# A two-layer diffusion trunk on one core: first-layer scale columns as full-width matmuls, the shift in halves, the last output tile in token halves

## The reference, cut to what matters

```python
for i in range(2):
    sh, sc, gt = split((silu(cond) @ ada_w[i] + ada_b[i]), 3)   # once for the 512 latent, once for the 256 context tokens
    h = rmsnorm(x, norm_g[i]) * (1 + sc) + sh
    # layer 0: fourier mixer, layer 1: retention mixer (both with a SiLU gate and an output projection)
    o = fourier_mixer(h, w_in, w_out)  if i == 0 else  retention_mixer(...)
    x = x + gt * o
return rmsnorm(x, final_g)              # (1, 512, 1024)
```

## Time and profile before

| | us |
|---|---|
| median of 3 runs | 1000.4 (1000.3, 1000.4, 2994.8) |
| the profiled execution | 998.61 |
| its span on the core | 996.8 |
| PE busy | 941.6 |
| DVE / ACT / POOL busy | 562.2 / 343.6 / 248.3 |

### The profile page before, as it was taken

How to read it: one execution, slowest core, us unless ns; L and a number is a source line. 1 busy time by engine, 2 the same in 40 slices (tenths; PEclk the granted TensorE clock), 3 DMA queues, 4 the chain that set the end, 5 groups by cost and what they waited for, 6 DMA issues and landing times.

```text
span 996.8 us, 12904 instructions
## 1 busy us (share of the span) xinstructions
PE 941.6 (94%) x4748; PEld 810.4 (81%) x4748; DVE 562.2 (56%) x804; ACT 343.6 (34%) x577; POOL 248.3 (25%) x244
## 2 busy tenths in 40 slices
PE   6969998999999999959999999999999999998993
PEld 6968998888888888847888888887888788877882
DVE  6485877899995332358334445426434544565344
ACT  7233334232314332334333334323333323452230
POOL 3337970475574000024100131013100410020001
PEclk9989999999999999989999999999999999998997
DMA  8473332555555211211221122202121121102212
GB/s 307 140 233 152 121 101 90 190 191 173 186 188 206 92 64 64 84 42 56 72 76 52 35 72 69 68 13 84 63 65 40 42 84 42 63 1 89 101 63 84
DMA packets 27864, 98.67 MB, mean 99 GB/s; under 512 B 3848, under 2 KB 4008, under 8 KB 27568
## 3 DMA queue, kind: packets, MB, share of 16 engines
q1 hardware_dynamic: 25792, 90.25, 27.1%
q0 software_dynamic: 2032, 7.89, 2.1%
HBM read 96.01 MB, written 2.10 MB: 98 GB/s over the span
## 4 chain that ended last, share of the span: by engine, by line
PE 87%; DVE 7%; DMA 2%; POOL 2%; ACT 1%; issue 1%; DVEq 0%; SPq 0%; POOLq 0%
PE banks L1541 28%; PE banks L1542 28%; PE banks L1543 27%; DMA raw<-stream 2%; PE banks L1594 2%; DVE hreg L1334 1%; POOL gate L625 1%; DVE xreg L1393 1%; DVE gate L1328 1%; DVE ring L1003 1%; DVE xreg L1533 0%; DVE gate L1358 0%; POOL gate L618 0%; POOL xreg L635 0%; PE banks L1783 0%
## 5 line engine op out<-in xcount | busy, mean ns | idle before, releaser
L1541 PE MATMUL banks<-hreg,ring 128*128 128x512 f32 (+2 forms) x928 | 334.1, 360 | 26.9 <-DVE hreg L1334 9.1
L1542 PE MATMUL banks<-hreg,ring 128*128 128x512 f32 (+2 forms) x928 | 331.8, 358 | 0.0
L1543 PE MATMUL banks<-hreg,ring 128*128 128x512 f32 (+2 forms) x928 | 329.2, 355 | 0.0
L1003 DVE TENSOR_TENSOR ring<-raw,ring 128x512 fp32r<-128x512 f32 x192 | 139.9, 745 | 271.5 <-ACT ring L662 270.8
L662 ACT ACTIVATE ring<-raw 128x512 fp32r<-128x512 f32 x192 | 119.3, 630 | 386.6 <-PE banks L1543 304.7
L1541 PEld LDWEIGHTS banks<-hreg,ring 128*128 128x128 f32 x928 | 176.6, 190 | 55.4 <-issue 12.8
L1543 PEld LDWEIGHTS banks<-hreg,ring 128*128 128x128 f32 x928 | 176.1, 190 | 23.3
L1542 PEld LDWEIGHTS banks<-hreg,ring 128*128 128x128 f32 x928 | 176.6, 190 | 22.3 <-issue 1.0
L585 POOL TENSOR_TENSOR gate<-xreg,gate 128x257 f32<-128x257 f32 (+1 forms) x64 | 76.1, 1219 | 74.0 <-ACT gate L794 57.9
L1035 DVE CUSTOM_DVE_ANT_0 dist<-raw,gate 128x1024 bf16<-128x1024 f32 x64 | 85.8, 1341 | 3.8
L618 POOL TENSOR_TENSOR gate<-gate 128x512 f32<-128x512 f32 x12 | 16.8, 1397 | 250.7 <-ACT gate L868 249.9
(11 more groups left out here) (205 smaller groups left out, 1117.5 us busy)
## 6 DMA issues: line engine op xcount, KB each, us to landing
raw<-stream SPq DMA_DIRECT2D x160, 512.0 KB, 3.3
gate<-x_rows SPq DMA_DIRECT2D x6, 512.0 KB, 6.8
gate<-x_lat POOLq DMA_DIRECT2D x1, 2048.0 KB, 9.5
...
```

What stands on the lines that cost most here:

```text
L1003: dve.tensor_tensor(ring[:, n % 2, 1, c], raw[:, buf, c], f32(ring[:, n % 2, 0, c]), ALU.subtract).then_inc(split_done, 1)
L1541: pe.matmul(out, left[0], right[0], start=start, stop=False)
L1542: pe.matmul(out, left[0], right[1], start=False, stop=False)
L1543: return pe.matmul(out, left[1], right[0], start=False, stop=stop)
```

## The change

At the start:

- All eight scale tiles come first on PE, and the shift tiles 0 to 3 are now D, 4 to 7 are P (`DVE_SHIFT = 4`): four dots on DVE and four tiles on PE. `ada_tile` streams the two condition columns 64 times (`WARM = 64`), 128 columns instead of 2, and its results take every 128th pair of two banks.
- The low part of the DFT tables and the two first `fold_diff` go from DVE to POOL; the identity matrix gets memory of its own and is made at the very start; POOL's `decay_first` waits until `xs` is made. One scaling of a token row goes from DVE to ACT.
- DVE adds the shift in two halves, `add_shift(0, 4)` after block 4 and `add_shift(4, 8)` after block 7. PE starts group 0 of U when blocks 0 to 6 are out and the first half is in, and asks for the second half at its fifth row tile.

At the end:

- The last output tile is computed as two halves of 256 tokens. The sum of squares of the first half is taken while PE works on the second, as columns: `token_sum` has the squares as weights and one column of ones, so that root and reciprocal work on 128x2 numbers; `token_rows` spreads them again over 128 partitions with a matmul against a diagonal matrix, once for DVE (which then reads it from a bank) and once for POOL (through ACT).
- The outputs are scaled and stored by halves, in six transfers with rows of 1 KB.

```diff
-START = "PPPPPPPPDPDPDPDD"
-PE_SHIFT = 3
+START = "PPPPPPPPDPDPDPDP"
+DVE_SHIFT = 4
+WARM = 64
...
@@ sync
-            for m in range(KT):
-                if m < POOL_TILES:
-                    sp.wait_ge(out_pool, m + 1)
-                    src = tmp_t[:, m, 0:LAT]
-                else:
-                    sp.wait_ge(out_vec, m - POOL_TILES + 1)
-                    src = x3[:, m, :]
-                sp.dma_start(out[m], src).then_inc(s_out, 16)
+            for h in range(2):
+                c = slice(LAT // 2 * h, LAT // 2 * (h + 1))
+                for a, b in ((POOL_TILES, 6), (6, KT)):
+                    sp.wait_ge(out_vec, (KT - POOL_TILES) * h + b - POOL_TILES)
+                    sp.dma_start(out[a:b].rearrange("m p t -> p m t")[:, :, c],
+                                 x3[:, a:b, c]).then_inc(s_out, 16)
+                    if h == 0 and b == 6:
+                        sp.wait_ge(out_pool, POOL_TILES)
+                        sp.dma_start(out[0:POOL_TILES].rearrange("m p t -> p m t")[:, :, c],
+                                     tmp_t[:, 0:POOL_TILES, c]).then_inc(s_out, 16)
@@ gpsimd
+            for i, (a, b) in enumerate(((0, 2 * NB), (2 * NB, DFT_COLS))):
+                pool.wait_ge(tab_hi, i + 1)
+                pool.tensor_tensor(tables[1][:, a:b], xreg[:, FEAT_COLS + a:FEAT_COLS + b],
+                                   f32(tables[0][:, a:b]), ALU.subtract).then_inc(tab_lo, 1)
             pool.wait_ge(s_x[TT - 1], 16)
             for v in range(2):
                 pool.dma_start(cond_rows[:, v, :], ...).then_inc(s_cond, 16)
+            pool.wait_ge(xs_lo, 6)
             pool.wait_ge(s_decay, 16)
             decay_first()
...
-            fold_sum(0)
-            fold_sum(1)
+            for n in range(2):
+                fold_sum(n)
+                fold_diff(n)
...
+            for h in range(2):
+                pool.wait_ge(rstd_done, 3 + h)
+                for m in range(POOL_TILES):
+                    pool.wait_ge(gained, m + 1)
+                    pool.tensor_tensor(tmp_t[:, m, c], tmp_t[:, m, c], rstd_t[:, c],
+                                       ALU.mult).then_inc(out_pool, 1)
@@ scalar
             x_root(4)
+            act.wait_ge(tok_rstd_done, 5)
+            act.activation(x_tok[:, 4, :], x_tok[:, 4, :], ACT.Copy,
+                           scale=tok_rstd[:, 4:5]).then_inc(xa_done, 1)
             x_root(5)
...
+            for h in range(2):
+                act.wait_ge(x2_half, h + 1)
+                act.activation(sq_t[:, 1, c], x3[:, KT - 1, c], ACT.Square).then_inc(sq_half, 1)
+                act.wait_ge(sum_sq_done, 3 + h)
+                act.activation(tok_rms[:, 2 * h:2 * h + 2], src, ACT.Sqrt, ...).then_inc(end_root, 1)
+                act.wait_ge(rows_spread, 2 * h + 2)
+                act.activation(rstd_t[:, c], bank(3 + 2 * h, LAT // 2), ACT.Copy).then_inc(rstd_done, 1)
+            act.wait_ge(out_pool, 2 * POOL_TILES)
+            act.dma_start(out[0:POOL_TILES]...[:, :, c], tmp_t[:, 0:POOL_TILES, c]).then_inc(s_out, 16)
@@ vector
+            early(KT)
             for k in range(KT):
                 transform_lo(k)
-                if k in dots_after:
-                    early(dots_after[k])
-                if k == KT - 2:
-                    fold_diff(0)
-                    fold_diff(1)
+                if k < DVE_SHIFT - 1:
+                    early(KT + 2 * k + 2)
+                if k == 4:
+                    dve.wait_ge(early_dot, 2 * DVE_SHIFT)
+                    add_bias(mod0[:, 0:DVE_SHIFT, :], row_mod[:, :, :], ...)
+                    dve.wait_ge(ada_used, 2 * KT - DVE_SHIFT)
+                    add_bias(mod0[:, DVE_SHIFT:KT, :], pe_columns(7), ...)
+                    add_shift(0, DVE_SHIFT)
+                if k == 5:
                     fold_lo(0)
+            add_shift(DVE_SHIFT, KT)
             fold_lo(1)
...
-            dve.wait_ge(root_done, 3)
-            dve.reciprocal(rstd_t[:, 0:LAT], rstd_t[:, 0:LAT]).then_inc(rstd_done, 1)
-            dve.wait_ge(rstd_done, 3)
+            def token_rstd(h):
+                dve.wait_ge(end_root, h + 1)
+                r = tok_rms[:, 2 * h:2 * h + 2]
+                link(dve.reciprocal(r, r))
+                dve.tensor_tensor(spread[:, 2 * h:2 * h + 2, :],
+                                  ident[:, :].unsqueeze(1).to_broadcast([P, 2, P]),
+                                  r.unsqueeze(2).to_broadcast([P, 2, P]),
+                                  ALU.mult).then_inc(spread_done, 1)
+            def last_out(h, m):
+                dve.wait_ge(rows_spread, 1 + 2 * h)
+                dve.scalar_tensor_tensor(out=x3[:, m, c], in0=x3[:, m, c], scalar=g_final[:, m:m + 1],
+                                         in1=bank(1 + h, LAT // 2), op0=ALU.mult, op1=ALU.mult)
@@ tensor
-                    last = pe.matmul(o, raw[:, buf, P * k:P * k + P], csf[:, k:2 * KT:KT],
+                    last = pe.matmul(o, raw[:, buf, P * k:P * k + P],
+                                     csf[:, k:2 * KT:KT].unsqueeze(1).to_broadcast([P, WARM, 2]),
                                      start=k == 0, stop=k == KT - 1)
...
+                    if g == 0:
+                        pe.wait_ge(shift_done, s + 1)
...
-            pe.wait_ge(shift_done, 1)
+            pe.wait_ge(hf_lo, 2 * (KT - 1))
             project_u(0)
...
-            pe.wait_ge(acc_done, 3 * KT + 5)
-            pe.matmul(bank(0), ones[:, :], acc_t[:, 0:LAT], start=True, stop=True).then_inc(sum_sq_done, 1)
+            for h, o in enumerate((bank(6, LAT // 2), bank(4, LAT // 2))):
+                for kk in range(FT):
+                    last = mm3(o, part_of(...), (g1(kk, 0)[:, c], g1(kk, 1)[:, c]), ...)
+                    if h == 1 and kk == 5:
+                        pe.wait_ge(acc_half, 1)
+                        for i in range(2):
+                            last = token_sum(bank(0, 1, i), i, (acc_t,))
+                        last.then_inc(sum_sq_done, 1)
+                    if h == 1 and kk == 11:
+                        token_rows(0)
+                if h == 0:
+                    last.then_inc(last_half, 1)
+            token_sum(bank(6, 1), 2, (acc_t, squares7))
+            token_sum(bank(7, 1), 3, (acc_t, squares7)).then_inc(sum_sq_done, 1)
+            token_rows(1)
```

190 lines of the change are left out of this document (119 added, 71 removed).

## The result

The changed kernel takes 984.45 us (median of five, 983.73 to 989.9) where the kernel before takes 1001.45 on the same chip: a ratio of 0.984, 95% interval 0.9814 to 0.9867. One of the five runs of the kernel before took 2994.8 us; the ratio leaves it out, and so left its median is 1000.9. The forecast was 983.3 with a range of 978.5 to 989, and within 2%.

The account below looks back on a forecast made before the run. PE was taken as the bound, carrying 87% of the path; -10.3 (earlier U), -1.2 (warm U) and -5.6 (end) sum to -17.1 us, from the median 1000.4 to 983.3 us, range 978.5 to 989.

Parts of the forecast that it names:

- forecast -11.5: Start: U beginning at 62.5 instead of 72.77 us (-10.3), and U starting warm (-1.2).
- forecast -5.6: End: halved last tile, column root and half stores bring the span's end from 996.8 to 991.2 us; bounds 3 to 7.
- from 19.66 five tiles of 1.9 end at 29.2: Scale tiles ahead of block 0: wide columns keep PE's clock high, so five end at 29.2; before, three ended at 29.93.
- the 0.9 us set for the cold stretch: PE after the pause before slot 11: 3.65 us at half pace lose 1.8, of which half was counted.
- the forecast's pause: PE behind block 1: slot 11 lands at 40.7 us, about 4 us after PE has finished that block.
- the forecast's -10.3: Start of U's first matmul: 62.5 us against 72.77 in the profile before.
- U's cold start (-1.2): U's group 0 on PE: 48 matmuls took 9.85 us, 8.6 at full pace; starting warm saves 1.2 us.
- no wait worth counting: Inside U's first group: second shift half and `fold_lo(1)` end about 65.5, when PE still has 4.2 us of first-half work from 61.6.
- Tables on POOL late: Start: DVE's two-input work and POOL's subtractions hold each other up, adding 3.2 us; U near 65.7, 986.5 us; chance 0.20.
- Everything holds: Start and end: clock never falls, slots take 3.1 us, U starts at 60.8, end gives -6.3; 980.9 us; chance 0.20.
- Start given back in U: U, 62 to 160 us: a late fold, table or `x_lat` costs 3 to 6 us; 987 to 989; chance 0.06.
- Load and stream don't overlap: Scale tiles and last tile: exposed weight loads add 16.4 us, 1016.8; result turns at some four fifths exposed; chance 0.04.

Follow-up runs that it names:

- shift_one: The changed kernel, but PE waits for both halves of the shift before the first U group; ratio 0.9878 to the kernel before.
- cond_dot_first: The changed kernel, with POOL issuing the condition rows before its table subtractions and DVE running the first row dots before `fmul`; ratio 0.9814 to the kernel before.
- tables_dve: The changed kernel with both table subtractions back on DVE, so POOL issues the condition rows right behind its casts; ratio 0.9812 to the kernel before.
- again: The changed kernel once more, without an edit, for a second profile; 987.55 us, ratio 0.9842 to the kernel before.
- deep_slots: The changed kernel with condition rows issued before POOL's subtractions and slots 3 to 5 landing in idle columns of `xreg`; 981.35 us, ratio 0.9789 to the kernel before.
- narrow: The changed kernel with WARM = 1, so scale and shift tiles on PE stream 2 columns again; 992.8 us, ratio 0.9911 to the kernel before.

## Why the prediction was right, and where it was not

The time was right, 983.3 against 984.45, and so was the cut: by the medians the start gives -10.1 (forecast -11.5) and the end -4.35 (forecast -5.6), together -14.5, while the change itself measured -17.0 (-16.5 without the run of 2994.8 us) and, once more, -14.4 against the forecast's -17.1. That the first median came within 1.2 us is in part luck: two errors inside the sum partly offset each other.

**What held.** A wide tile takes 1.88 us at the high clock (5.63 / 3) and 3.4 at the low one. The condition rows were ready at 34.25 (33.8): POOL was quicker than I took it for (3.07, not 4.2), the transfer slower. U no longer waits for the shift; the halves are worth 3.8 us (shift_one). Most of the end: DVE takes the second half over 13.0 us behind the last tile's start, 1.9 later than before (2.0); a scaling is 0.41; POOL's branch is the last; the store takes 2.9 (3.3). The largest part of what is missing of -5.6 is the second spreading of the rows on PE: it takes 2.08 us for 8 half-products where the first took 1.05, at a granted clock of 0.50 behind two waits of 1.12 and 1.01 us; I had 0.9. The shorter store gives 0.4 back.

**The step that failed: "from 19.66 five tiles of 1.9 end at 29.2", and with it the 0.9 us set for the cold stretch.** Block 0 starts at 36.06 in the change and at up to 37.13 in three more profiles of this start; in shift_one it is 32.72. Two terms were too small.

*The waits.* I took a slot's landing as late only at slot 11 and let the tiles ahead of block 0 run freely. With tiles of 1.9 us instead of 3.5, a freed buffer gives the next slot two tiles, 3.8 us, until PE asks for it, and the median landing of 4.9 is longer: a wait could have been seen in the rows on hand. But the three buffers don't cause it alone. Slot 6 landed in 3.2 us and PE didn't wait for it; slot 7 met the condition rows and took 7.2. With the rows out of its way and the same buffers, PE waits 0 and 0.6 us ahead of block 0 (cond_dot_first, tables_dve). I had moved the rows behind POOL's subtractions and priced only when they come, not what they meet.

*The pace.* From 19.84 to U it is 48.5 us: nine tiles and eight blocks need 37 at the upper level, the waits for two slots 5.67 (3.75 and 1.92), and the other 6 are what some 12 us of work at 1.2 GHz lose (behind 20.9, 32.6 and 51.6). Against the forecast's pause, 4.5 us by its own numbers, the waits are only 1.2 us more, and the wait for slot 11 itself didn't come; against its 0.9 the pace is 5 us more. In this profile, then, the clock behind the waits is the larger miss. In again the waits are as long, 5.3, and the clock falls twice instead of three times; in shift_one it never falls, and PE is done at 62.1.

U is at 65.3 to 68.4 in four profiles of this start instead of 62.5, and in the median run near 64.7 by the estimate above. deep_slots takes both the waits ahead of block 0 and the falls away and gets U at 59.00.

**The error on the other side** was the base. I measured from 72.77, the U of one lucky execution; the others of the old start are at 73.97 and 77.91. From their mean of 74.9 to the 66.7 of the new start it is -8.2 us, less than the forecast's -10.3. The medians have -10.1; the profiles of the change and of again are of their slowest runs, and with U near 64.7 in the median run it is -10.2, an estimate.

**U's cold start (-1.2)** hardly came: from U to the end of PE's wait of 2.60 us it is 89.40 where it was 89.76 us, since the second half's `fold_lo` costs 0.68 that I had called no wait worth counting. The mechanism is real: in shift_one, where PE stands ahead of U and has no 0.68 to wait, that stretch is 90.04, that is 1.3 us longer than 89.40 less 0.68.

**The rivals.** "Tables on POOL late" had the right place, in a mild form: 2.31 instead of 1.28 for the fold, and rows that meet a slot. By tables_dve against again it is worth 3 us in the ratio (0.9812 to 0.9842, overlapping intervals). "Everything holds" came nearest in shift_one, where the clock stays up and PE is done at 62.1 (60.8 in the rival). "Start given back in U" didn't come: the later waits of PE are those of before, line by line. "Load and stream don't overlap" is ruled out by the 1.88. Its "four fifths of a load" doesn't follow from its own ends: from -17.1 with none of a load exposed to +16.4 with all of it, the turn lies near a half.

The Trainium skill ("TensorE: Matmul & The Clock Gate", LDWEIGHTS section) gives a weight load as columns / 1.2 in ns and names no clock for it, so 107 ns for 128 columns. By that an estimate for narrow's tiles of 16 half-products is 1.7 us; they take 3.53 here, 0.22 per half-product, up to 36.8 us, and 0.11 later. The trace disagrees, as it did before.
